# The seventh down chunk of each network by seven products, its sums added up by transfers within SBUF

## What is computed

```
x = x + jnp.square(jax.nn.relu(h @ w_up[l])) @ w_down[l]          # first network, hidden width 4096
return rms_norm(x, norm_final)                                    # then the second network starts
...
hid = jnp.square(jax.nn.relu(jnp.einsum('bsd,df->bsf', n2, w_up[l])))
mlp_out = jnp.einsum('bsf,fd->bsd', hid, w_down[l])
h = h + rms_norm_2(mlp_out, norm_mlp_post[l])                     # the end of the kernel
```

## Time and profile before

| | us |
|---|---|
| median of 3 runs | 1567.31 (1567.03 to 1567.4) |
| profiled execution, its time | 1567.51 |
| profiled execution, its span | 1565.7 |
| TensorE busy | 1549.0 (99%) |
| VectorE busy | 987.3 (63%) |
| ScalarE busy | 662.7 (42%) |
| GpSimd busy | 482.6 (31%) |

### The profile page before, as it was taken

One profiled execution on the slowest core, in us unless ns is written; L12 is line 12 of the kernel. 1 busy time (PEld: TensorE's weight loads), 2 busy tenths in 40 slices (PEclk: granted clock), 3 DMA queues, 4 the chain that ended last, 5 costly groups with the idle time before them and its releaser, 6 DMA issues.

```text
span 1565.7 us, 21038 instructions
## 1 busy us (share of the span) xinstructions
PE 1549.0 (99%) x7752; PEld 1303.1 (83%) x7752; DVE 987.3 (63%) x1188; ACT 662.7 (42%) x1092; POOL 482.6 (31%) x282
## 2 busy tenths in 40 slices
PE   8999999999999999999999999999999999999998
PEld 6888888888788888888888898988888988888886
DVE  5454876435477776876664747357356677777765
ACT  5352665244444443443533433643334453434342
POOL 2451000000037776752300000020013047767732
PEclk9999999999999999999999999999999999999999
DMA  6422136221313233215332132243334332213133
GB/s 247 150 70 79 41 108 191 79 81 54 135 54 108 108 108 107 107 55 160 89 106 83 55 95 71 92 162 105 111 124 147 135 108 102 89 45 135 67 116 120
DMA packets 44997, 164.35 MB, mean 105 GB/s; under 512 B 5584, under 2 KB 5784, under 8 KB 44272
## 3 DMA queue, kind: packets, MB, share of 16 engines
q1 hardware_dynamic: 40608, 144.82, 28.4%
q0 software_dynamic: 4304, 18.38, 3.4%
HBM read 158.89 MB, written 5.85 MB: 105 GB/s over the span
## 4 chain that ended last, share of the span: by engine, by line
PE 93%; DVE 4%; ACT 2%; DMA 1%; issue 1%; SPq 0%; DVEq 0%; ACTq 0%
PE banks L1235 29%; PE banks L1237 29%; PE banks L1236 29%; PE banks L1534 1%; PE banks L1413 1%; DVE nmax L2230 1%; DVE w_lo L1944 1%; DMA w_raw<-in_weights 1%; PE banks L1352 0%; PE banks L1596 0%; DVE banks L2229 0%; PE banks L1572 0%; PE banks L1564 0%; PE banks L1523 0%; DMA x_tok<-in_x 0%
## 5 line engine op out<-in xcount | busy, mean ns | idle before, releaser
L1235 PE MATMUL banks<-act_hi,w_hi 128*128 128x512 f32 (+1 forms) x1088 | 413.7, 380 | 3.1 <-DVE act_lo L2112 3.1
L1237 PE MATMUL banks<-act_hi,w_lo 128*128 128x512 f32 (+1 forms) x1088 | 410.3, 377 | 0.0
L1236 PE MATMUL banks<-act_lo,w_hi 128*128 128x512 f32 (+1 forms) x1088 | 410.2, 377 | 0.0
L1944 DVE TENSOR_TENSOR w_lo<-w_raw,w_hi 128x1024 fp32r<-128x1024 f32 x216 | 280.0, 1303 | 203.2 <-ACT w_hi L1632 199.8
L1632 ACT ACTIVATE w_hi<-w_raw 128x1024 fp32r<-128x1024 f32 x216 | 227.0, 1059 | 251.6 <-DMA w_raw<-in_weights 196.8
L1235 PEld LDWEIGHTS banks<-act_hi,w_hi 128*128 128x128 f32 x1088 | 204.9, 188 | 40.8 <-DVE w_lo L1944 1.6
L1237 PEld LDWEIGHTS banks<-act_hi,w_lo 128*128 128x128 f32 x1088 | 204.9, 188 | 37.7
L1236 PEld LDWEIGHTS banks<-act_lo,w_hi 128*128 128x128 f32 x1088 | 205.0, 188 | 36.4
L1235 PE MATMUL banks<-w_hi,a_hi 128*128 128x512 f32 x400 | 155.8, 389 | 0.0
L1237 PE MATMUL banks<-w_hi,a_lo 128*128 128x512 f32 x400 | 155.7, 389 | 0.0
L1236 PE MATMUL banks<-w_lo,a_hi 128*128 128x512 f32 x400 | 155.7, 389 | 0.0
(11 more groups left out here) (367 smaller groups left out, 2393.4 us busy)
## 6 DMA issues: line engine op xcount, KB each, us to landing
w_raw<-in_weights SPq DMA_DIRECT2D x216, 512.0 KB, 3.7
w_down<-in_weights SPq DMA_DIRECT2D x48, 512.0 KB, 6.4
wide<-share_dram POOLq DMA_DIRECT2D x3, 1024.0 KB, 10.2
x_tok<-in_x SPq DMA_DIRECT2D x4, 512.0 KB, 5.2
w_first<-in_weights SPq DMA_DIRECT2D x4, 512.0 KB, 8.5
x_tok<-in_x POOLq DMA_DIRECT2D x4, 512.0 KB, 5.0
x_dram<-x_tok POOLq DMA_DIRECT2D x1, 2048.0 KB, 8.1
x_tok<-x_dram POOLq DMA_DIRECT2D x1, 2048.0 KB, 8.5
```

Of the source, the lines that this page charges most:

```text
L1235: pe.matmul(out_ap, lhs[0], rhs[0], start=start, stop=False)
L1236: pe.matmul(out_ap, lhs[0], rhs[1], start=False, stop=False)
L1237: return pe.matmul(out_ap, lhs[1], rhs[0], start=False, stop=stop)
L1944: dve.tensor_tensor(w_lo[:, slot, :], landed(kind, raw), w_hi[:, slot, :], ALU.subtract).then_inc(lo_w, 1)
```

## The change

The function `seven` also takes the seventh down chunk, in both networks: 84 matmuls in place of 96, with the weight sums on GpSimd and seven weight splits in the last up product. `products(last=True)` places its seven products in the bank pairs 4, 6, 0, 2, 4, 6, 2; the copies of the eighth chunk's activations (`whole`) come before its first product. The special copy of one part goes away.

The fold moves out of the last up product, behind the products, one piece at each as it is ready. Six of the eight pieces are transfers from SBUF to SBUF, issued by GpSimd, that add to their target (`fold_by_dma`): x11 += q1 behind product 1, q6 += q1 behind 2, x22 += q5 behind 3 (in the second network a plain copy), q7 += q6 and, when that has landed, x22 += q7 behind 4, x21 += q7 behind 6. Two stay on VectorE behind product 6: x12 += q5 and x12 += q6. VectorE waits for the transfers at the additions into tile 0, 1 and 2, GpSimd at its multiplications in the first network. `load2` and `unpark` are issued behind product 2's piece. The x that comes back in the second network goes to a place of its own, `x_late`, where `w_down` was, and the output is stored from there.

```diff
--- before.py
+++ after.py
@@ -111,7 +111,7 @@
 def seven(g):
 
     name, row0 = GROUPS[g][:2]
-    return name in ("w_down", "w_down_2") and row0 < FF - 2 * T
+    return name in ("w_down", "w_down_2") and row0 < FF - T
 
 
 UNITS = ("b11", "b21", "t2", "t1", "t3", "b22", "t4")
...
@@ -385,10 +386,14 @@
         place = {u.slot: j for j, u in enumerate(self.mine)}
         ends = []
         squared = self.count("sq", 0)
-        sums = self.add("sums", counts={"sum_a": 4}, sq=squared, held=self.count("lo_a", 0)).sum_a
-        held = self.count("lo_a", 7)
+        if last:
+            sums, held = None, self.count("lo_a", 4)
+            self.add("whole", held=held, sq=squared)
+        else:
+            sums = self.add("sums", counts={"sum_a": 4}, sq=squared, held=self.count("lo_a", 0)).sum_a
+            held = self.count("lo_a", 7)
         for j in range(7):
-            bank = 4 + 2 * (j % 2)
+            bank = (4, 6, 0, 2, 4, 6, 2)[j] if last else 4 + 2 * (j % 2)
             banks = (bank, bank + 1)
             splits = []
             for u in self.coming:
@@ -396,9 +401,9 @@
                 if after + 1 == j:
                     splits.append(self.split_of(u, [ends[after]] if after >= 0 else [(3, self.fills_of(3))]))
             ends.append((bank + 1, self.cell(self.fills[bank + 1] + 1, ("bank", bank + 1))))
-            yield self.add("product", banks, n=j, dst=dst, first=first, splits=splits,
+            yield self.add("product", banks, n=j, dst=dst, first=first, last=last, splits=splits,
                            units=[self.placed(self.mine[j])], held=held, of=ends, sum_a=sums, sq=squared)
-        self.last_bank = 5
+        self.last_bank = bank + 1
 
 
 def at(count, turn, plus=0):
...
@@ -565,14 +571,13 @@
             up()
             down()
         s.end_loop()
-        s.add("whole", held=s.count("lo_a", 1), sq=s.count("sq", 0), dst="parts")
-        up(after="fold")
-        after_last()
-        steps = s.bank_steps("add", "tok", "parts", rows=4, halves=2, dst=dst)
-        go(steps, 1)
-        s.add("whole", held=s.count("lo_a", 4), sq=s.count("sq", 0), dst="act")
-        go(steps, 16)
-        s.add("unpark", ready=ready(), dst=dst)
+        up()
+        for st in s.products(dst, last=True):
+            taken = filled_by(st)
+            s.add("fold", n=st.n, ready=taken, dst=dst)
+            if st.n == 2:
+                after_last(taken)
+                s.add("unpark", ready=taken, dst=dst)
         last(s.bank_steps("add", "tok", "act", rows=4, halves=2, dst=dst, by_tile=True))
 
     for tt in range(TT):
@@ -761,7 +766,7 @@
         go(s.project0, 4)
 
     s.gemm("up", "T", "act", ready=act_ready, pairs=True)
-    run_mlp("x", lambda: s.add("load2", ready=all_out()), first_end)
+    run_mlp("x", lambda taken: s.add("load2", ready=taken), first_end)
     go(s.project0, 16)
     for p in range(PATTERNS):
         s.gemm("v2", "tok", "act", p=p)
...
@@ -1723,11 +1737,8 @@
                 elif k == "whole":
                     act.wait_ge(sq_made, at(st.sq, turn))
                     act.wait_ge(lo_a, at(st.held, turn))
-                    if st.dst == "parts":
-                        act.activation(a_hi[:, 2], sq[:, 0:2, low_], ACT.Copy).then_inc(hi_a, 1)
-                    else:
-                        for c in range(4):
-                            act.activation(act_hi[:, c, :], sq[:, c, :], ACT.Copy).then_inc(hi_a, 1)
+                    for c in range(4):
+                        act.activation(act_hi[:, c, :], sq[:, c, :], ACT.Copy).then_inc(hi_a, 1)
                 elif k == "split":
                     split(st, turn)
                 elif k == "parts":
...
@@ -1986,6 +1986,9 @@
                     col0 = 512 * (st.half if st.rows == 4 else st.blk)
                     if st.after == "x_back":
                         dve.wait_ge(x_back[st.nth], 16)
+                    if st.rows == 4:
+                        for name in {(0, 0): ("x11",), (1, 1): ("q7",), (2, 0): ("x21",), (2, 1): ("x22_q5", "x22")}.get((st.nth, st.half), ()):
+                            dve.wait_ge(fold_in[name], FOLDED[st.dst])
                     part = dst[:, st.nth, col0:col0 + 512]
                     dve.tensor_tensor(part, psum[:, b, :], part, ALU.add).then_inc(bank_free[b], 1)
                 elif st.out == "up":
@@ -2028,6 +2031,8 @@
                     gemm(st, turn)
                 elif k == "split":
                     split(st, turn)
+                elif k == "fold":
+                    fold(st)
                 elif k == "product":
                     dst = {"x": x, "y": y}[st.dst]
                     for t, b in enumerate(st.banks):
@@ -2082,7 +2087,7 @@
                         dve.wait_ge(x_again, 16)
                         for half in range(2):
                             part = slice(512 * half, 512 * half + 512)
-                            dve.scalar_tensor_tensor(x[:, tt, part], xg[:, tt, part], r, x[:, tt, part], ALU.mult, ALU.add
+                            dve.scalar_tensor_tensor(x_late[:, tt, part], xg[:, tt, part], r, x_late[:, tt, part], ALU.mult, ALU.add
                                                      ).then_inc(out_made, 1)
                 elif k == "guard":
                     signal, count = st.made
@@ -2398,18 +2403,16 @@
                     pool.tensor_tensor(t4[:], w_down[:, 2, :], t2[:], ALU.subtract).then_inc(sum_w, 1)
                 elif k == "sums":
                     block_sums(pool, st, turn)
-                elif k == "product":
+                elif k == "product" and not st.last:
                     for j in (st.n - 1, st.n) if st.n == 6 else (st.n - 1,):
                         if j >= 0:
                             part_lo(pool, st, j, turn)
                 elif k == "whole":
-                    pool.wait_ge(hi_a, at(st.held, turn, 1))
-                    if st.dst == "parts":
-                        pool.tensor_tensor(a_lo[:, 2], sq[:, 0:2, low_], a_hi[:, 2], ALU.subtract).then_inc(lo_a, 1)
-                    else:
-                        for c in range(4):
-                            pool.wait_ge(hi_a, at(st.held, turn, c + 1))
-                            pool.tensor_tensor(act_lo[:, c, :], sq[:, c, :], act_hi[:, c, :], ALU.subtract).then_inc(lo_a, 1)
+                    for c in range(4):
+                        pool.wait_ge(hi_a, at(st.held, turn, c + 1))
+                        pool.tensor_tensor(act_lo[:, c, :], sq[:, c, :], act_hi[:, c, :], ALU.subtract).then_inc(lo_a, 1)
+                elif k == "fold":
+                    fold_by_dma(st)
                 elif k == "gemm":
                     if st.out == "merge" and (st.half, st.bank) != (1, TT - 1):
                         b = st.bank
@@ -2458,14 +2461,14 @@
                     wait_ready(pool, st.ready, turn)
                     pool.dma_start(x_dram, x[:].rearrange("q t d -> q (t d)")).then_inc(parked, 16)
                 elif k == "unpark" and st.dst == "y":
-                    pool.wait_ge(fold_made, 2)
-                    wait_ready(pool, st.ready[0:1], turn)
-                    pool.dma_start(x[:].rearrange("q t d -> q (t d)"), x_dram).then_inc(x_again, 16)
+                    wait_ready(pool, st.ready, turn)
+                    pool.dma_start(x_late[:].rearrange("q t d -> q (t d)"), x_dram).then_inc(x_again, 16)
                 elif k == "square" and st.half == 0:
                     wait_ready(pool, st.ready, turn)
                     pool.wait_ge(row_in, 16 * st.row_n)
                     if st.mode == "final":
-                        pool.wait_ge(fold_made, 1)
+                        for name in {0: ("x11", "q6"), 1: ("q7",), 2: ("x22_q5",), 3: ("x22", "x21")}[st.n]:
+                            pool.wait_ge(fold_in[name], 16)
                     src = x if st.mode == "final" else y
                     pool.tensor_tensor(gained[st.mode][:, st.n, 0:512], src[:, st.n, 0:512], row[:, 0:512], ALU.mult).then_inc(xg_first, 1)
                 elif k == "apply":
@@ -2513,6 +2516,29 @@
                     for p in range(PATTERNS):
                         pool.dma_start(wide[p][:].rearrange("q t h -> q (t h)"), share_dram[p].partition_broadcast(P)).then_inc(wide_in[p], 16)
 
+            def fold_by_dma(st):
+
+                q, (x11, x12, x21, x22) = sums_of[st.dst], quarters(st.dst)
+                done = FOLDED[st.dst]
+                if st.n in (1, 2, 3, 4, 6):
+                    wait_ready(pool, st.ready, None)
+                if st.n == 1:
+                    pool.dma_start(x11, q["q1"], accum_op=ALU.add).then_inc(fold_in["x11"], 16)
+                elif st.n == 2:
+                    pool.dma_start(q["q6"], q["q1"], accum_op=ALU.add).then_inc(fold_in["q6"], 16)
+                elif st.n == 3 and st.dst == "y":
+                    pool.dma_start(x22, q["q5"]).then_inc(fold_in["x22_q5"], 16)
+                elif st.n == 3:
```

(10 more changed lines are left out.)

47 lines of the change are left out of this document (22 added, 25 removed).

## The result

| | before | after |
|---|---|---|
| median of the same comparison, us | 1567.37 | 1582.97 (1582.08 to 1583.69) |
| ratio | | 1.0099, interval 1.0088 to 1.0110 |
| profiled execution: time, span, us | 1567.51, 1565.7 | 1582.08, 1580.3 |
| mean granted clock | 0.999 | 0.992 |

What follows compares the result with a forecast made beforehand. TensorE was taken to bound the kernel; -5.44 + 0.1 + 5.2 + 0.2 = +0.1 us gave 1567.4 us, with 1562.2 to 1576 to hold it 8 times in 10. The forecast case had chance 0.36.

Steps and rivals of the forecast that it cites:

- What bounds: Whole kernel: TensorE is busy for 99% of the span, so time is saved only where it does less or waits less.
- part 1: Seventh down chunk, both networks: seven products of 12 matmuls instead of 96 matmuls save 2.72 us per network, 5.44 us for both.
- part 2: Fold leaving the up product: removing its additions gains nothing; two returning on VectorE behind product 6 cost 0.1 us.
- t = 0: The end of the last matmul of the seventh down chunk, taken separately in each network; t counts us from there.
- Part 3: The six transfers and who waits for them: GpSimd's wait for q7 delays tile 0, costing 5.2 us in the first network.
- Q: Landing time of q7 after the last product: forecast 9.5 us in the first network, 5.8 in the second; costs above 4.3.
- a: Cost of one 512 KB fold transfer on its queue: taken as 1.6 us, between 1.0 and 2.8.
- the sign that I had named: Landing of an adding transfer that is alone: 4 us or less means the gain stays, over 5.5 us speaks for rival 2.
- rival 2: Adding transfers hold the engines twice as long, at q7 (first network) and x21 (second): +7.9 us, 1575.2; chance 0.31.
- From Q to the transposes: First network, two issues, multiplication, chain to the scaling, scaling and handover to TensorE: 1.1 + 1.3 + 3.5 + 1.3 + 0.1 = 7.3 us.
- The second network: End of the kernel: VectorE is held 0.5 us for x21 at tile 2, with idle time behind; cost 0.2 us.
- rival 3: Traffic holds the last weight tiles of the eighth down chunk, then 1580; chance 0.03 together with the rest.

## Why the prediction was wrong

- **What bounds, part 1, part 2: right.** The chunk takes 19.04 us and TensorE is busy in it; without the fold the gain is 4.8 us of the 5.44. Of part 2, the plain copies leave the two additions on VectorE, and their second network ends 28.3 us behind t = 0, as without any fold; for the first network no run takes them by themselves.
- **Part 3, the mechanism: right.** GpSimd's wait for q7 sets when tile 0 starts, and the formula for Q holds: with the measured price 15.5 for 16.0 (first network), 8.3 for 8.6 (plain copies), and 10.3 for 10.9 (second: 1558.59 - 1547.64). Nor is that luck: from 727.5 to 751.3 q0 and q1 were busy for 73.3% and 19.8% of the 16 engines, 22.2 us, where the formula adds up 12.4 + 5.9 + 4.0 = 22.3. One wait was missing from it: q7 was issued at t = 2.6 and not at -2.7, as GpSimd first waits 4.36 us for q6 to land. It cost nothing, because the queue had load2 and x22 += q5 to work off meanwhile.
- **The step that failed is the price *a*.** I took 1.6 us, the weight tile's rate, between 1.0 and 2.8; it is 3.0 to 3.1 (the sign that I had named, landings over 5.5 us, is there too: 6.1 and 6.6). Four transfers in Q, so 6 us of Q. This is rival 2, to which I gave 0.31 against 0.36; even its own figure of 2.8 was short, and its 1575.2 with it. The weight tile's row was the most frequent one, but it was no nearer to an adding transfer than twice the plain one, which was the reasoned bound. The argument against, that a transfer within SBUF does not touch the outer memory, was worth next to nothing: the plain copies within SBUF cost 1.3, against 1.4 for the reload from DRAM.
- What the Trainium skill says of sums in "Collectives: The Full Stack" (two sources read, half the rate) is said of ReduceScatter, another operation; for transfers that add within SBUF the runs go the same way and a little further, 1.3 and 3.0 us. It had stood beside the forecast as a hint for rival 2, and no row of before was near enough to speak against it.
- **From Q to the transposes I had 7.3 us; it is 9.0.** The two issues take from 751.30 to 753.72, if the multiplication is 1.3 us at the end of its row, which overlaps the second issue (2.23 = 0.93 + 1.3): 2.4 us, not 1.1; the two plain issues of the copies took 1.5. The scaling is 1.75, not 1.3. Together 1.7.
- **The clock was no term at all.** A wait of 13.9 us sends TensorE back at 1.2 GHz, the lower level (0.50 at 759.5 to 761.9): 2.9 us more. The forecast's own wait of 5 us would have brought some of it too: behind 5.59 us (plain copies) the granted clock is 0.50 from 750 to 755.
- **The second network: 0.2 forecast, 4.3 measured.** I asked only when x21 and x22 reach VectorE, and reckoned with GpSimd's first multiplication behind the wait for q7 in the first network alone. It is behind it in both, and in the second that wait comes first; rival 2's place, x21 at tile 2, is the next in line (3.55 us once the other is gone). I had also read the earlier trace rows one addition too early: 1551.14 is the first addition into tile 2, so x21 is needed at t = 13.8 and x22 at 16.8, not at 11.1 and 13.8. With my own Q neither would have cost anything, and rival 2's 6.5 us there would have been 3.8.
- **Weights late (rival 3) was real but small**, 1.4 us of TensorE's wait and 0.9 us of the median without the fold. In after the first split is at 740.52 too, hidden under the wait.
- The range ended at 1576 because it stopped at a = 2.8. The sum with all that is measured, -5.44 + 13.4 + 2.9 + 4.3 = 15.2, meets the 15.6.

## What to carry to other kernels

An addition folded into a transfer is not free work on idle engines: count it at more than two plain transfers, add all that stands ahead of it on its queue, and ask which issuing engine then waits for it and what is queued behind that wait. Work that was hidden in one stage must be priced anew where it goes, here 19.8 us for a gain of 4.8. And before sharing work with GpSimd, look whether VectorE runs instructions with two SBUF inputs beside it.

## What the runs showed that I had not expected

- An adding transfer within SBUF: 3.0 to 3.1 us of the 16 engines for 512 KB, against 1.3 plain; landings 6.6 against 4.2 us in the same place.
- VectorE's instruction with two SBUF inputs beside GpSimd's: 6.71, 3.23 and 2.77 us for 1.3, 1.2 and 0.7. The scaling that took 2.40 us in the kernel before fits it: it ends 1.1 us behind the end of GpSimd's multiplication (747.96 to 749.26).
- TensorE after a wait: granted clock 0.50 after 13.9 us (2.9 us lost), and in part after waits of 3.1 to 3.7 us (0.50 for 750 to 755, and 0.73). A short wait can cost clock on top of its length, but the length alone does not tell: a wait of 2.35 us at the transposes cost none (they took 1.09 us as before, with the last two transfers behind tile 0), one of 2.29 us did (0.73 over 745 to 750, all additions on VectorE).
